# The second mixer's input products: memory panels, two norms and the memory's heads in one stage, and a later start for GpSimd's shift

## What is computed

```python
    return rms_norm(x, final_norm)              # end of first_block
    ...
        u = _rms_norm(h, norm_mix_w[layer])     # start of second_block
        proj = u @ w_in[layer]                  # 1024 x 9232
        xbc = jax.nn.silu(_causal_depthwise_conv(xbc, ssd_conv_w[layer], ssd_conv_b[layer]))
        ...
        mkv = _rms_norm(mem, mem_norm_w[layer]) @ w_mem_kv[layer]     # 1024 x 1536
        mk = mkv[..., :MEM_WIDTH].reshape(b, n_mem, MEM_HEADS, MEM_HEAD_DIM)
        mv = mkv[..., MEM_WIDTH:].reshape(b, n_mem, MEM_HEADS, MEM_HEAD_DIM)
        mk = _rms_norm(mk, mem_k_norm_w[layer])
```

## Time and profile before

| | us |
|---|---|
| median of 3 runs | 3737.91 |
| lowest and highest run | 3737.23, 3740.41 |
| profiled execution, its own time | 3741.4 |
| span of its trace | 3739.6 |
| PE busy in the span | 3452.9 (92%) |
| DVE busy | 2537.6 (68%) |
| ACT busy | 1882.7 (50%) |
| POOL busy | 78.7 (2%) |

### The profile page before, as it was taken

The page is one execution under the profiler, slowest core; times in us unless marked ns, Lnnn a source line. Parts: engine busy times, 40 slices in busy tenths (PEclk is TensorE's granted clock), DMA queues, the critical chain, the costliest instruction groups (busy, mean ns, idle before and its releaser), DMA issues. The chain is left out here.

```text
span 3739.6 us, 54504 instructions
## 1 busy us (share of the span) xinstructions
PE 3452.9 (92%) x21788; PEld 3063.0 (82%) x21788; DVE 2537.6 (68%) x3059; ACT 1882.7 (50%) x2014; POOL 78.7 (2%) x51
## 2 busy tenths in 40 slices
PE   5999899999897799999999998898787999999999
PEld 5978789989787588778877777896587999977887
DVE  7857466388555588888888873644654887495665
ACT  3533444263433476766767662543343444464454
POOL 1000000010000000000000000000000000000000
PEclk9999899999998799999999999999898999999999
DMA  7720356368012499999999983352042555404554
GB/s 264 276 97 1 113 214 233 126 215 294 6 68 79 151 365 367 360 364 361 368 363 361 364 326 113 136 191 86 1 148 89 181 184 180 164 1 154 194 191 157
DMA packets 291525, 739.15 MB, mean 198 GB/s; under 512 B 12817, under 2 KB 12818, under 8 KB 285586
## 3 DMA queue, kind: packets, MB, share of 16 engines
q1 hardware_dynamic: 291346, 736.69, 55.4%
HBM read 735.59 MB, written 1.05 MB: 197 GB/s over the span
## 5 line engine op out<-in xcount | busy, mean ns | idle before, releaser
L2098 DVE TENSOR_TENSOR weight_ring_low<-weight_ring,weights_high 128x2048 fp32r<-128x2048 f32 x336 | 773.4, 2343 | 129.7 <-ACT weights_high L2044 129.7
L2044 ACT ACTIVATE weights_high<-weight_ring 128x2048 fp32r<-128x2048 f32 x336 | 618.6, 1906 | 9.7 <-DMA weight_ring<-in_moe_w 9.7
L437 PE MATMUL psum_all<-h_high_projections,high_projections 128*128 128x256 f32 x1536 | 435.5, 284 | 17.4 <-DVE h_low_projections L326 10.9
L437 PE MATMUL psum_all<-h_low_projections,high_projections 128*128 128x256 f32 x1536 | 432.2, 281 | 0.0
L437 PE MATMUL psum_all<-h_high_projections,weight_ring_low 128*128 128x256 f32 x1536 | 431.7, 281 | 0.0
L1986 PE MATMUL psum_all<-weights_high,expert_in_turn_high 128*128 128x512 f32 x896 | 358.7, 400 | 18.1 <-POOL expert_in_turn_low L1930 16.5
L1986 PE MATMUL psum_all<-weights_high,expert_in_turn_low 128*128 128x512 f32 x896 | 353.8, 395 | 0.0
L1986 PE MATMUL psum_all<-weight_ring_low,expert_in_turn_high 128*128 128x512 f32 x896 | 353.6, 395 | 0.0
L437 PEld LDWEIGHTS psum_all<-h_high_projections,high_projections 128*128 128x128 f32 x1536 | 290.9, 189 | 21.8 <-DVE h_low_projections L326 13.8
L3014 PE MATMUL psum_all<-peer_h_high,expert_rows_high 128*128 128x256 f32 x1024 | 291.1, 284 | 5.0 <-DVE expert_rows_low L3062 5.0
L514 DVE TENSOR_TENSOR weight_ring_low<-weight_ring,high_projections 128x2048 fp32r<-128x2048 f32 x96 | 215.8, 2286 | 115.2 <-ACT high_projections L468 115.2
(11 more groups left out here) (611 smaller groups left out, 7884.2 us busy)
## 6 DMA issues: line engine op xcount, KB each, us to landing
weight_ring<-in_moe_w SPq DMA_DIRECT2D x336, 1024.0 KB, 5.1
weight_ring<-in_w_in SPq DMA_DIRECT2D x48, 2048.0 KB, 8.6
expert_rows<-in_peer_down SPq DMA_DIRECT2D x128, 512.0 KB, 3.2
expert_rows<-in_peer_up SPq DMA_DIRECT2D x128, 512.0 KB, 3.2
weight_ring<-in_ffn_halves SPq DMA_DIRECT2D x42, 1024.0 KB, 6.2
branch_out<-in_ada_w SPq DMA_DIRECT2D x64, 512.0 KB, 10.0
weight_ring<-in_w_out SPq DMA_DIRECT2D x6, 2048.0 KB, 8.3
weight_ring<-in_ada_w SPq DMA_DIRECT2D x4, 2048.0 KB, 13.8
```

What stands on the lines that cost most here:

```text
L437: mm = pe.matmul(half(k.ps, 4 * (g % R) + j), w[:, c, j * P:(j + 1) * P], x[:, c], start=(c == 0 and n == 0), stop=(c == KC - 1 and n == 2 ...
L2044: act.activation(high[:, q, h * HALF:(h + 1) * HALF], k.ring[:, q, h * HALF:(h + 1) * HALF], ACT.Copy).then_inc(high_made[q], 1)
L2098: dve.tensor_tensor(k.low[:, q, part], k.ring[:, q, part], high[:, q, part].bitcast(F32), ALU.subtract).then_inc(low_made[q], 1)
```

## The change

One stage, `second_projections`, takes the place of `memory_projections`, `memory_heads` and `projections2`. Its panels are the memory's three and then the mixer's eighteen, in one ring. Working space lies in blocks of the output that are written late. `NSIG` goes from 32 to 42. In `shifts` POOL waits once, for all eight chunks.

```diff
-NSIG = 32
+NSIG = 42
...
     def shifts(self, pool):
         if self.shift is not None:
+            pool.wait_ge(self.split, KC)
             for c in range(KC):
-                pool.wait_ge(self.split, c + 1)
                 pool.tensor_scalar(self.h[:, c], self.h[:, c], self.shift[:, c:c + 1], None, ALU.add)
```

`memory_keys`, `memory_heads` and the argument `beside` of `project` go. Of the new function (the bodies of `split`, `low`, `product` and of the convolution are those of `project`):

```diff
+def second_projections(k, mk, mv, dest, dest_at):
+    H, R_MEM, C0, CN = 2, 3, 5, 4
+    FIRST_SUMS, FIRST_TURN, FIRST_SPREAD, LAST_SPREAD, LAST_TURN = 10, 11, 12, 13, 14
+    KEYS = 52
...
+        panels = [(first + i, KEYS + 4 * i) for i in range(R_MEM)]
+        panels += [(k.start["in2_a"] + i, 4 * i) for i in range(6)] + [(k.start["in2_b"] + i, 24 + 4 * i) for i in range(12)]
...
+            def _(pool):
+                st.clear_last(pool)
+                pool.memset(rs_keys[:], 0.0).then_inc(prepared, 1)
+                pool.tensor_copy(pairs[:], col_bc(k.ident[:, 0:MH], 64)).then_inc(prepared, 1)
...
+            def _(pe):
+                mem.sums(pe)
+                final.sums(pe)
+                for i, (g, blk) in enumerate(panels):
+                    x = mem if i < R_MEM else nm
+                    if i >= R:
+                        pe.wait_ge(copied, i - R + 1)
...
+                        for j in range(4):
+                            for c in range(KC):
+                                if i == R_MEM and j == 0:
+                                    pe.wait_ge(nm.split, c + 1)
+                                if j == 0 and c % 4 == 0:
+                                    pe.wait_ge(low_made, 2 * i + c // 4 + 1)
+                                mm = product(j, c)
+                            if i == 1 and j == 2:
+                                nm.sums(pe)
+                    mm.then_inc(k.used, 1)
+                    if i == FIRST_SUMS:
+                        sums()
+                    if i == FIRST_TURN:
+                        pe.wait_ge(keys_mean, 1)
+                        turns((0, 1, 2))
+                    if i == FIRST_SPREAD:
+                        pe.wait_ge(prepared, 2)
+                        pe.wait_ge(keys_inverse, 1)
+                        pe.wait_ge(moved, 3)
+                        spreads((0, 1, 2, 3))
+                    if i == LAST_SPREAD:
+                        pe.wait_ge(keys_done, 2)
+                        spreads((4, 5))
+                    if i == LAST_TURN:
+                        pe.wait_ge(keys_done, 6)
+                        turns((3, 4, 5))
...
+            def _(act):
+                mem.squares(act)
+                act.wait_ge(k.loaded[first % R], k.load_value(first))
+                split(0, 0)
+                mem.roots(act)
+                final.squares(act)
+                split(0, 1)
+                mem.highs(act)
+                final.roots(act)
+                for i in range(1, n_all + 1):
+                    if i < n_all:
...
+                        for n in range(2):
+                            split(i, n)
+                    if i == 1:
+                        act.wait_ge(final.done, KC // 2)
+                        nm.squares(act)
+                    if i == 2:
+                        nm.roots(act)
+                        nm.highs(act)
+                    if i == FIRST_SUMS:
+                        act.wait_ge(copied, 2)
+                        for b in range(3):
+                            act.activation(sq_keys[:, 2 * b:2 * b + 2], keys[:, 2 * b:2 * b + 2], ACT.Square).then_inc(keys_squared, 1)
+                    if i == FIRST_SUMS + 2:
+                        act.wait_ge(keys_mean, 1)
+                        act.activation(rs_keys[0:MH], rs_keys[0:MH], ACT.Sqrt).then_inc(keys_root, 1)
+                    if i == FIRST_TURN + 2:
+                        act.wait_ge(turned, 1)
+                        moves((0, 1, 2))
+                    if i == LAST_TURN + 2:
+                        act.wait_ge(turned, 2)
+                        moves((3, 4, 5))
...
+                    g, blk = panels[i - 1]
+                    act.wait_ge(k.used, g + 1)
+                    if blk >= LATE:
+                        act.wait_ge(done, 4 * CN)
+                    if i > R_MEM and blk == KEYS:
+                        act.wait_ge(keys_done, 6)
+                        act.wait_ge(moved, 6)
+                    out = k.ps[:, 2 * (g % R):2 * (g % R) + 2, :].rearrange("p b (j t) -> p (b j) t", j=2)
+                    act.activation(dest[:, blk:blk + 4], out, ACT.Copy).then_inc(copied, 1)
...
+            def _(dve):
+                mem.folds(dve)
+                low(0, 0)
+                mem.means(dve)
+                mem.inverses(dve)
+                mem.blocks(dve, lambda: low(0, 1))
+                final.means(dve)
+                for i in range(n_all):
+                    if i > 0:
+                        low(i, 0)
+                        low(i, 1)
+                    if i == 1:
+                        final.blocks(dve)
+                        dve.wait_ge(final.done, KC)
+                        nm.folds(dve)
+                    if i == 2:
+                        nm.means(dve)
+                        nm.inverses(dve)
+                        nm.blocks(dve, lambda: None)
...
+                    if i == FIRST_SPREAD + 1:
+                        unit((0, 1, 2, 3))
+                    if i == LAST_SPREAD + 1:
+                        unit((4, 5))
```

More of the change, by code:

```diff
@@ L375, in blocks, with project @@
             dve.scalar_tensor_tensor(x, x, self.scale[:, c:c + 1], self.rs[:], ALU.mult, ALU.mult).then_inc(self.done, 1)
-def project(k, name, src, norm, parts, h, dest, ahead=R, conv=None, extra=None, beside=None):
+def project(k, name, src, norm, parts, h, dest, ahead=R, conv=None, extra=None):
     H = 2
@@ L2287 @@
 MEMORY_AT = 221152
[L2290 to L2302, removed]
+def second_projections(k, mk, mv, dest, dest_at):
+    H, R_MEM, C0, CN = 2, 3, 5, 4
+    HALF = SLOT // 2
+    LATE = 64
+    FIRST_SUMS, FIRST_TURN, FIRST_SPREAD, LAST_SPREAD, LAST_TURN = 10, 11, 12, 13, 14
+    KEYS = 52
@@ L2305, in heads, with place @@
     def heads(b):
         return b // 3 * 2 + b % 3 // 2, b % 3 == 1
[L2308 to L2314, removed]
-    with ExitStack() as ctx:
[L2317 to L2320, removed]
-            block = st.block
-            squared, summed, mean, root, inverse, spreaded, done, paired, cleared, turned, moved = st.signals(11)
+    def place(b):
+        return dest_at + 4 * T * b
@@ L2340, in _, with split @@
-            @block.tensor
-            def _(pe):
-                for b in range(6):
-                    pe.wait_ge(squared, b // 2 + 1)
-                    mm = pe.matmul(k.ps[0:MH, 3, 0:T], select(b), sq[:, b], start=(b == 0), stop=(b == 5))
-                mm.then_inc(summed, 1)
-                for b in range(6):
-                    for i in range(TT):
-                        mm = pe.transpose(half(k.ps, b)[:, i * P:(i + 1) * P], k.proj[:, 6 + b, i * P:(i + 1) * P], k.ident)
-                mm.then_inc(turned, 1)
-                pe.wait_ge(paired, 1)
-                pe.wait_ge(inverse, 1)
-                for b in range(6):
-                    pe.matmul(half(k.ps, 8 + b), spread(b), rs[:], start=True, stop=True).then_inc(spreaded, 1)
+                def split(i, n):
+                    g = panels[i][0]
+                    part = slice(n * HALF, (n + 1) * HALF)
+                    act.activation(high[:, i % H, part], k.ring[:, g % R, part], ACT.Copy).then_inc(high_made, 1)
@@ L2355, in _, with low @@
             @block.vector
             def _(dve):
[L2357 to L2365 removed]
+                def low(i, n):
+                    g = panels[i][0]
+                    part = slice(n * HALF, (n + 1) * HALF)
+                    dve.wait_ge(high_made, 2 * i + n + 1)
+                    dve.tensor_tensor(k.low[:, g % R, part], k.ring[:, g % R, part], high[:, i % H, part].bitcast(F32),
+                                      ALU.subtract).then_inc(low_made, 1)
```

153 lines of the change are left out of this document (116 added, 37 removed).

## The result

| | before | after |
|---|---|---|
| median of 5 runs, us | 3737.34 | 3714.98 |
| lowest and highest, us | 3735.84, 3740.41 | 3711.19, 3717.63 |
| profiled execution: time, span, us | 3741.4, 3739.6 | 3711.19, 3709.3 |

The ratio is 0.9947, 95% interval 0.9936 to 0.9958: 20 us faster, 16 to 24 (22.4 by the two medians).

A forecast was written before the change was run, and what follows sets the result against it. PE, busy 92% of the span, was taken as the bound. 21.3 - 6.4 - 1.3 + 0.6 = 14.2 us off the profiled 3741.4 left 3727.2; 3.5 less for the median gave 3723.7, range 3720 to 3730.5.

The forecast's parts named there:

- The seam: From the memory's first sums to `ssd_gates`: 22.8 us gained up to panel 4 at full clock, less 6.4 inserted.
- inserted work: Memory's heads behind panels 10 to 14, on PE's path: sums 2.5, spreads 2.5, transpositions 1.4, together 6.4 us lost.
- The cover of the heads' waits: Waits ahead of the heads' matmuls cost nothing; the tightest, the first spreading, has 6 us of cover.
- rivals 3 and 4: Heads' waits: 3, five places cost PE 7.5 us, chance 0.12; 4, queues chain again, 23.8 us, chance 0.04.
- the clock in the stall: At panel 3, the mixer's first, PE's stall brings the clock down: 1.5 us lost, between 0 and 2.5.
- rival 1: At panel 3 the clock holds through the stall: 1.5 us better, 3722.2 us, chance 0.27.
- the clears: Ten more semaphores delay POOL 0.64 us at the experts' start and the last mix: 1.3 us lost.
- the later shift: In each layer, DVE's multiplications without POOL's adds beside them: 0.3 us gained a layer, 0.6 in all.
- rival 2: POOL's adds slow panel 1's splits in both layers, 2 x 2 x 1.0 us: 4.6 worse, 3728.3 us, chance 0.10.

The follow-up runs named there:

- e2: Changed kernel with the shift in `shifts` as it was before the change: ratio to before 0.9964, median 3720.72 us.
- e4: Changed kernel run again with no edit: ratio to before 0.9952, median 3716.23 us.
- e7: Changed kernel, each stage clearing only as many semaphores as the one before took: 3709.51 us, one run.
- e11: Changed kernel run again with no edit, for more runs: ratio to before 0.9958, median 3717.94 us.
- e12: e2 run again with no edit: ratio to before 0.9961, median 3718.45 us.
- e5: Changed kernel with the final norm's sums behind panel 0, as before the change: 3723.67 us, one run.
- e10: Changed kernel with one extra 128x2048 copy on ACT ahead of its split of panel 3: 3720.77 us, one run.
- e8: Changed kernel with two extra 128x2048 copies on ACT ahead of its split of panel 3: 3719.10 us, one run.
- e1: Kernel before with the later shift alone (POOL waits once for all chunks): ratio to before 0.9997, median 3733.06 us.
- e3: Kernel before with ten more semaphores alone (`NSIG = 42`): ratio to before 1.0001, median 3735.04 us.
- e9: Changed kernel with the edits of e6 and e7 together: ratio to before 0.9938, median 3712.01 us.
- e6: Changed kernel with ACT's first split of panel 3 moved into ACT's wait between the norm's root and first high part: 3711.22 us, one run.

## Why the prediction was right or wrong

**The seam was right but for the clock.** Its terms were 22.8 us up to panel 4 (clock held) less 6.4 of inserted work, 16.4; the rows show 278.85 - 262.44 = 16.4. That it fits to a tenth is luck: up to panel 4 the gain was 23.2, because the mixer's first panel could start 0.4 us earlier than worked out, and the inserted work took 6.8 for 6.4, 0.3 of it in the sums. In the clock of the new trace, 9.2 us ahead of the old from the stages before, the forecast had panel 1 at 2302.2 (2302.1 measured), panel 3 at 2328.6 (2328.2) and panel 4 at 2340.7 (2340.35). The cover of the heads' waits held; rivals 3 and 4 fall by the missing idle time.

**First failed step: the clock in the stall.** The forecast took it to fall, at 1.5 us, because it had fallen in the dense layer around a wait of 2.27 us. It held in the changed kernel, e2, e4, e7, e11 and e12, and in e5 after a wait of 2.28 us; it fell when e10 made the wait 3.36 us. In the dense layer it fell in all fourteen profiles, behind waits of 2.25 to 3.01 us. So that row was no like case: the wait there was followed by sparse work, as rival 1 said, here by dense. That the work behind the wait decides is the likely reason, but no run changed it alone, and as one length can go either way (the 2.03 us above) e5's single profile is no proof. Rival 1 was the true one. The Trainium skill's warning of idle gaps (TensorE: Matmul & The Clock Gate, "Why this matters for your kernels") agrees with e8 and e10. 1.5 us.

**Second: the clears.** 0.64 us for each of two places was priced by when GpSimd starts, not by when PE ends. At the experts only 0.12 was lost. What PE waits for there is a GpSimd row that VectorE holds up. The rows of the kernel before:

```profile
1264.36 4.50 POOL L1930 TENSOR_TENSOR expert_in_turn_low<-expert_tokens,expert_in_turn_high 128x1024 fp32r<-128x1024 f32 x1
1266.56 4.44 DVE L2098 TENSOR_TENSOR weight_ring_low<-weight_ring,weights_high 128x2048 fp32r<-128x2048 f32 x1
```

GpSimd's subtraction began 6.10 us behind PE's last matmul in the kernel before, 6.31 in e1 and 6.45 in e3, and in all the profiles but e7 and e9 it ended 2.2 us after the end of VectorE's first split. That split took 2.29 us in the kernel before and e1, 2.40 to 2.42 with the longer list of clears, and this is the 0.12. In e7 GpSimd began 1.9 us ahead of it and took 2.35. VectorE's second split took 4.44 us beside GpSimd's subtraction, 2.28 without it. At the mix 0.35 to 0.92 was lost, 0.64 in the changed kernel, and most of it given back by the clock, which rose no later; 0.76 more came from the last eight matmuls. The runs of e3 are too coarse to say what the clears cost in all; by its profile the two places together lost nothing. 1.3 us, or a little more.

**Third: the later shift**, 0.3 for a layer, was 0.44 to 0.46. The mechanism was as told, its sizes were not: DVE got 0.94 us back in the chunks (0.9 forecast), the sums beside the adds gave up 0.29 (0.6), and the second split of panel 1 another 0.20 (nothing). Rows of DVE and PE in layer 0 after the change, to set beside the earlier trace rows:

```profile
50.43 0.48 DVE L319 SCALAR_TENSOR_TENSOR hidden_in<-residual,mod,rs_projections 128x256 f32<-128x256 f32 x1
...
56.99 4.47 DVE L641 SCALAR_TENSOR_TENSOR modulation_sums<-branch_out,c_act,modulation_sums 128x512 f32<-128x512 f32 x5
61.39 4.68 DVE L515 TENSOR_TENSOR weight_ring_low<-weight_ring,high_projections 128x2048 fp32r<-128x2048 f32 x2
```
```profile
54.36 0.39 PE L444 MATMUL psum_all<-h_high_projections,high_projections 128*128 128x256 f32 x1 [0.30 <-DVE h_low_projections L326]
...
66.12 0.38 PE L444 MATMUL psum_all<-h_high_projections,high_projections 128*128 128x256 f32 x1 [0.72 <-DVE weight_ring_low L515]
```

The multiplication is back at 0.48 us, the five sums take 4.47 us for 4.18, and PE still waits for the split at 66.12. Under the adds the two splits took 2.28 and 2.48 us. The Trainium skill (GPSIMD Engine Reference, "Specifications") names VectorE instructions with two SBUF inputs as those that contend with GpSimd. The traces agree for the split too, 0.20 us here in place of the 1.0 for each of rival 2, and 2.16 us at the experts' start. It is GpSimd that pays here: beside the splits two of its adds took 3.03 and 2.51 us, beside the sums 0.92 to 1.09. The prediction read the interference "only for the multiplications"; the row of 4.44 us was in the same trace. 0.3 us in all.

**Fourth: base and range.** The forecast started from a median of three runs, 3737.9; the mean of 39 is 3735.3. That is 2.6 us. And the range took no account of how far the untouched 3450 us of the program wander with the clock: six to nine microseconds between profiles, 14 between runs.

3723.7 - 1.5 - 1.3 - 0.3 - 2.6 = 3718.0. The mean of 16 runs is 3716.8, within its error of 1.5. That the first comparison showed 22 us by the medians is chance on top: a second and a third gave 17.6 and 17.8. Whether a microsecond of it is an effect of the change on when the clock falls in later stages is open. The stretch from queries to values speaks for some effect: 76.8 to 77.4 us in the seven profiles of the changed kernel, e2, e4, e5, e7, e11 and e12, 78.5 to 79.3 in the kernel before, e1 and e3, but 78.8 to 79.2 also in e6, e8, e9 and e10, where the seam was shorter or longer by 2.4 us and more. Against it stands e5, whose seam was 3.1 us longer and which is among the first: the length of the seam doesn't sort them. That the clock's changes lie at random against the work was not tested in itself; that they lie elsewhere from run to run is shown.

## What to carry to other kernels

Chains of short steps between two stages are worth their whole idle time when they are laid beside the panels of one stage, and such a gain can be worked out to half a microsecond from in-order queues and row durations. Look then at the first place where the two queues meet: here one split, moved into a wait on its own engine, gave 2.4 us more. Ask of an engine that another waits for not only when it starts but what its rows lie beside: GpSimd's start moved by 0.35 us and its end by 0.12. A forecast of the total needs the spread of the untouched part: compare stretch by stretch between the same instructions before a difference of spans is believed.

## What the runs showed of the hardware

- Runs of this program without any change lie between 3728 and 3742 us, and most of that goes with the granted clock. PE's time at the lower level outside of the seam was 235 to 261 us in the fourteen profiles.
- The length of a wait alone did not decide whether the clock fell. It held at panel 3 with waits of 1.6 and 0.6 us (six profiles) and with 2.28 (e5), and fell there with 3.36 and 5.17, for 0.7 and 1.4 us in all. It fell after 2.03 us in ten cases of 28 in the layers, after 1.64 us at the last mix of e7 and e9, where the eight matmuls behind the wait read one partition each, and without any wait in the same eight matmuls at the end of the kernel before and e1.
- Delaying the first matmul behind a long wait by 0.35 to 0.64 us did not delay the clock's rise; by the mix's 400th matmul -0.1 to 0.3 us of the delay was left.
- GpSimd's subtraction of 128x1024 took 4.50, 4.27 or 2.35 us. In e7, with the shortest, it began 1.9 us ahead of DVE's split, which then took 2.60 us for 2.29; in the others it began with or behind that split, and the next split took 4.44 us for 2.28. Each of the two engines waited for the other.
